# Up projection of a conv-MLP: 19 of 22 channel pairs by seven half-size block products, activation kept in DRAM

## What is computed

```python
h = rms_norm(x, norm_ffn_pre[l])
up = causal_dwconv(jnp.einsum('bsd,df->bsf', h, ffn_w_up[l]), ffn_conv_w[l]) + ffn_conv_b[l]
gate, val = jnp.split(up, 2, axis=-1)
ff = jnp.einsum('bsf,fd->bsd', jax.nn.silu(gate) * val, ffn_w_down[l])
x = x + rms_norm(ff, norm_ffn_post[l])
```

## Time and profile before

| | us |
|---|---|
| three runs: median, lowest, highest | 1058.16, 1056.17, 1058.37 |
| span of the profiled execution | 1058.0 |
| TensorE busy in it | 1044.1 |
| VectorE, ScalarE busy | 492.0, 335.3 |

### The profile page before, as it was taken

The page is one execution under the profiler, slowest core; times in us unless marked ns, Lnnn a source line. Parts: engine busy times, 40 slices in busy tenths (PEclk is TensorE's granted clock), DMA queues, the critical chain, the costliest instruction groups (busy, mean ns, idle before and its releaser), DMA issues.

```text
span 1058.0 us, 12361 instructions
## 1 busy us (share of the span) xinstructions
PE 1044.1 (99%) x4808; PEld 850.6 (80%) x4808; DVE 492.0 (47%) x537; ACT 335.3 (32%) x525; POOL 30.8 (3%) x82
## 2 busy tenths in 40 slices
PE   8999999999999999999999999999999999999997
PEld 7988777768888888888888888888887888888886
DVE  5637776554553443434434343343444233344454
ACT  5425444443332312213121231212223222333342
POOL 2100000001110000000000000000000000000001
PEclk9999999999999999999999999999999999999999
DMA  6521010053232111211112111121211322343343
GB/s 209 146 60 39 23 40 28 33 172 107 94 106 67 57 57 40 59 40 45 54 40 59 40 50 49 40 59 40 79 40 59 100 97 81 99 160 127 131 139 119
DMA packets 75390, 81.59 MB, mean 77 GB/s; under 512 B 2793, under 2 KB 62433, under 8 KB 75361
## 3 DMA queue, kind: packets, MB, share of 16 engines
q1 hardware_dynamic: 75233, 81.13, 24.3%
q0 software_dynamic: 128, 0.07, 0.0%
HBM read 72.80 MB, written 8.39 MB: 77 GB/s over the span
## 4 chain that ended last, share of the span: by engine, by line
PE 95%; DMA 2%; DVE 1%; ACT 1%; issue 0%; POOL 0%; SPq 0%; DVEq 0%; POOLq 0%; ACTq 0%
PE ps L1133 30%; PE ps L1135 30%; PE ps L1134 30%; PE ps L1143 1%; PE ps L1241 1%; DMA xin<-in_x 1%; PE ps L1264 1%; PE ps L1242 1%; PE ps L1250 1%; DMA wraw<-in_w_o 1%; PE ps L1268 1%; DVE hlo L761 0%; PE ps L1279 0%; POOL rstd L449 0%; ACT hhi L486 0%
## 5 line engine op out<-in xcount | busy, mean ns | idle before, releaser
L761 DVE TENSOR_TENSOR wlo<-wraw,whi 128x1024 fp32r<-128x1024 f32 x98 | 120.0, 1224 | 404.6 <-ACT whi L486 404.5
L1133 PE MATMUL ps<-h2hi,whi 128*128 128x512 f32 x704 | 277.5, 394 | 0.0
L1135 PE MATMUL ps<-h2hi,wlo 128*128 128x512 f32 x704 | 276.0, 392 | 0.0
L1134 PE MATMUL ps<-h2lo,whi 128*128 128x512 f32 x704 | 273.2, 388 | 0.0
L486 ACT ACTIVATE whi<-wraw 128x1024 fp32r<-128x1024 f32 x98 | 103.8, 1059 | 513.6 <-PE ps L1135 509.0
L1135 PEld LDWEIGHTS ps<-h2hi,wlo 128*128 128x128 f32 x704 | 132.2, 188 | 30.9
L1134 PEld LDWEIGHTS ps<-h2lo,whi 128*128 128x128 f32 x704 | 132.1, 188 | 29.5
L1133 PEld LDWEIGHTS ps<-h2hi,whi 128*128 128x128 f32 x704 | 132.4, 188 | 26.2
L1133 PE MATMUL ps<-whi,ahi 128*128 128x512 f32 x320 | 126.7, 396 | 0.3 <-DVE alo L1052 0.3
L1135 PE MATMUL ps<-whi,alo 128*128 128x512 f32 x320 | 126.6, 395 | 0.0
L1134 PE MATMUL ps<-wlo,ahi 128*128 128x512 f32 x320 | 126.5, 395 | 0.0
(11 more groups left out here) (135 smaller groups left out, 1015.6 us busy)
## 6 DMA issues: line engine op xcount, KB each, us to landing
wraw<-in_ffn_w_up SPq DMA_DIRECT2D x44, 512.0 KB, 3.8
wraw<-in_ffn_w_down SPq DMA_DIRECT2D x44, 512.0 KB, 3.3
wraw<-in_w_in SPq DMA_DIRECT2D x14, 512.0 KB, 3.9
xin<-in_x SPq DMA_DIRECT2D x8, 512.0 KB, 4.5
wraw<-in_w_o SPq DMA_DIRECT2D x8, 512.0 KB, 3.3
xres<-in_x SPq DMA_DIRECT2D x8, 512.0 KB, 4.1
x_dram<-x2b SPq DMA_DIRECT2D x8, 512.0 KB, 2.9
x2f<-x_dram SPq DMA_DIRECT2D x8, 512.0 KB, 4.1
```

The source lines that it names most:

```text
L761: dve.tensor_tensor(lo[:, slot, :], wraw[:, base % RAW, :], hi[:, slot, :], ALU.subtract).then_inc(w_split, 1)
L1133: pe.matmul(acc, w_hi, x_hi, start=first, stop=False, skip_group_check=looped)
L1134: pe.matmul(acc, w_hi, x_lo, start=False, stop=False, skip_group_check=looped)
L1135: return pe.matmul(acc, w_lo, x_hi, start=False, stop=last, skip_group_check=looped)
```

## The change

Three pairs stay as they were. For the other 19 the pair's product is taken as one of 2 x 2 blocks: token halves by k halves (four blocks of the input) times k halves by gate and value (four blocks of the weight). It is multiplied by seven products (Winograd's form of Strassen's scheme), each one token half, one k half and one block of 128 output channels: 4 x 3 = 12 matmuls of 128x512.

- **Input side.** Four differences of quarters of the input (`r_full`, 128x2048 each) are made once on VectorE, between and after the plain pairs, and rounded and split (`r_hi`, `r_lo`).
- **Weight side.** For each pair VectorE makes four sums of weight quarters (`sum_weights`: one pass of 1024, two of 512); plain and summed quarters are rounded and split as four entries (three of 1024, one of 512) in a ring of six slots (`entry`): `w2hi`, a part of `h2hi` that is read no more, and `whi`.
- **Product side.** Some products serve two outputs. ScalarE copies PSUM to SBUF three times a pair (`keep`, 512 wide), VectorE adds it back to a bank three times (`fold`, 512 wide). TensorE waits before product 3 for the first copy, before product 5 for the third, before product 7 for the second fold. The value comes out negated: its bias is negated (`neg_bias`) and the last product has the factor -1.
- **Activation.** `act_raw` is gone. `yv` has two slots; each finished 128x1024 goes to `act_dram`. The down stage loads 128x512 pieces into a ring of four (`act_in`), the first two early into `gain_a`. `act_in` lies over the input differences, so those loads wait for the last product.
- The loop over pairs is written out on every engine.

The core of the diff:

```diff
+PLAIN = 3
+SEVEN = NF - PLAIN
+RING = 6
+ENTRY_LAST = (4, 5, 6, 7)
...
+            def load_pair(p):
+                for val in range(2):
+                    n = UP0 + 2 * p + val
+                    if p - 2 < PLAIN:
+                        sp.wait_ge(w_split, n - RAW + 1)
+                    else:
+                        sp.wait_ge(u_split, 4 * (p - 2 - PLAIN) + 4)
...
+            def save_act(p):
+                sp.wait_ge(act_ready, p + 1)
+                sp.dma_start(act_dram[p * P:(p + 1) * P, :], yv[:, p % 2, :])\
+                  .then_inc(act_saved[p % 2], 16)
...
+            for p in range(2, NF):
+                load_pair(p)
+                if p >= 3:
+                    save_act(p - 3)
...
+            def keep(q, which):
...
+                act.wait_ge(seven_done, 7 * q + which + 1)
+                if which == 0:
+                    act.wait_ge(act_ready, pair - 1)
+                if which == 2:
+                    act.wait_ge(act_saved[pair % 2], 16 * (pair // 2))
+                out = (yg[:, pair % 2, 0:HALF], yg[:, pair % 2, HALF:], yv[:, pair % 2, 0:HALF])[which]
+                act.activation(out, ps[:, (v0, g1, v0)[which], :], ACT.Copy).then_inc(kept, 1)
...
+            plain_step(0)
+            plain_step(1)
+            round_difference(0)
+            round_entry(0, 0)
+            round_entry(0, 1)
+            plain_step(2)
+            round_difference(1)
+            round_difference(2)
+            round_entry(0, 2)
+            round_entry(0, 3)
+            round_difference(3)
+            for q in range(SEVEN):
+                if q >= 1:
+                    start_value(q - 1)
+                    start_silu(PLAIN + q - 1)
+                if q + 1 < SEVEN:
+                    round_entry(q + 1, 0)
+                for which in range(3):
+                    keep(q, which)
+                if q + 1 < SEVEN:
+                    for i in range(1, 4):
+                        round_entry(q + 1, i)
...
+                start_gate(q)
...
+            def fold(q, which):
...
+                dve.wait_ge(seven_done, 7 * q + 4 + which)
+                dve.wait_ge(kept, 3 * q + 1 + which)
...
+                dve.tensor_tensor(ps[:, (g0, v1, g1)[which], :], ps[:, (g0, v0, g1)[which], :], part,
+                                  ALU.add).then_inc(folded, 1)
...
+            for q in range(SEVEN):
+                pair = PLAIN + q
+                g0, g1, v0, v1 = pair_banks(pair)
+                pe.wait_ge(up_freed, 2 * pair - 2)
+                seventh(q, 1, 0, 0, block_of(h2hi, 0), block_of(h2lo, 0), v0, True)
+                if q == 0:
+                    pe.wait_ge(r_split, 1)
+                seventh(q, 2, 1, 1, r_hi[0], r_lo[0], g1, True)
+                if q == 0:
+                    pe.wait_ge(r_split, 2)
+                pe.wait_ge(kept, 3 * q + 1)
+                seventh(q, 3, 2, 0, r_hi[1], r_lo[1], v0, False)
+                seventh(q, 4, 0, 1, block_of(h2hi, 1), block_of(h2lo, 1), g0, True)
+                if q == 0:
+                    pe.wait_ge(r_split, 3)
+                pe.wait_ge(kept, 3 * q + 3)
+                seventh(q, 5, 1, 0, r_hi[2], r_lo[2], v0, False)
+                seventh(q, 6, 2, 1, block_of(h2hi, 2), block_of(h2lo, 2), g1, False)
+                if q == 0:
+                    pe.wait_ge(r_split, 4)
+                pe.wait_ge(folded, 3 * q + 2)
+                seventh(q, 7, 3, 0, r_hi[3], r_lo[3], v0, False)
```

More of the change, by code:

```diff
@@ L669, in _ @@
             round_h(2 * NT - 1, h2hi)
[L671 to L677, removed]
-                    act.wait_ge(act_ready, pair - 1)
[L679 to L696, removed]
+            def plain_step(p):
+                j = p % 2
+                act.wait_ge(up_done, 2 * p + 1)
+                if p + 1 < PLAIN:
+                    round_weight(UP0 + 2 * p + 2, 0, whi, 0)
+                if p >= 2:
+                    act.wait_ge(act_ready, p - 1)
+                act.activation(yg[:, j, :], banks(4 * j), ACT.Identity, bias=ffn_bias(p),
+                               scale=ffn_tap(2, p)).then_inc(yg_started, 1)
+                act.wait_ge(up_done, 2 * p + 2)
+                if p + 1 < PLAIN:
+                    round_weight(UP0 + 2 * p + 3, 0, whi, 1)
+                if p >= 2:
+                    act.wait_ge(act_saved[j], 16 * (p // 2))
+                act.activation(yv[:, j, :], banks(4 * j + 2), ACT.Identity,
+                               bias=ffn_bias(p + NF), scale=ffn_tap(2, p + NF))\
+                   .then_inc(yv_started, 1)
+                start_silu(p)
@@ L698, in _, with round_act @@
+            def round_act(raw, hi, slot):
+                act.activation(hi[:, slot, :], raw, ACT.Copy).then_inc(a_rounded, 1)
             for q in x2_saved:
                 act.wait_ge(q, 16 * NT // 2)
[L700 to L707, removed]
@@ L719, in _ @@
             d1 = DOWN0 + NF
[L720 removed]
+            a1 = NF - 2
+            down_step(d1, 0, a1)
             for t in (0, 2):
@@ L1055, in low_act, with gate_taps @@
                    .then_inc(a_split, 1)
-            start = steps[0]
-            with dve.Fori(0, NF // 2 - 2) as it:
-                steps[0] = start + 4 * it
-                for j in range(2):
-                    up_step(it + 1, j)
-            steps[0] = start + 4 * (NF // 2 - 2)
-            up_step(NF // 2 - 1, 0)
-            for k in range(2):
-                low_act(k, k, 0, ahi, alo, k)
-            up_step(NF // 2 - 1, 1)
-            def down_step(base, q, k, half):
+            def gate_taps(p):
+                dve.wait_ge(yg_started, p + 1)
+                add_taps(yg[:, p % 2, :], banks(4 * (p % 2)), p)
@@ new lines, in made, with quarter, whole_quarter, low_difference @@
+            def made(i):
+                return r_full[i][:, :, :]
+            def quarter(i, lo):
+                return block_of(h2lo if lo else h2hi, i).rearrange("p t k c -> p t (k c)")
+            def whole_quarter(i, out):
+                return dve.tensor_tensor(made(out), quarter(i, False), quarter(i, True), ALU.add)
+            def low_difference(i):
+                dve.wait_ge(r_rounded, i + 1)
+                dve.tensor_tensor(r_lo[i][:, :, :, :].rearrange("p t k c -> p t (k c)"), made(i),
+                                  r_hi[i][:, :, :, :].rearrange("p t k c -> p t (k c)"),
+                                  ALU.subtract).then_inc(r_split, 1)
```

334 lines of the change are left out of this document (280 added, 54 removed).

## The result

| us | before | after |
|---|---|---|
| median of four runs each, taken side by side | 1058.26 | 1021.10 |
| lowest, highest | 1056.17, 1059.22 | 1019.89, 1022.97 |
| ratio of times, 95% interval | | 0.9645 [0.9627, 0.9663] |
| span of the profiled execution, its own time | 1058.0, - | 1018.1, 1019.89 |

The forecast was 1017.0, range 1011 to 1030. The time is 4.1 us above it, inside the range. In every execution of this study with both on record the time is 1.7 to 2.1 us longer than the span; this is the part around the span, and the forecast could not see it, since the time of before's profiled execution was not known. Before ran in all four, with medians of 1057.5 to 1058.3, so a difference of less than about 1 us between an experiment and the kernel after is no result.

The account below looks back on a forecast made before the run. TensorE, busy 99%, was taken as the bound, so only fewer matmuls save time. Span 1058.0 - 52.1 + 10.3 + 0.6 = 1016.8 us, plus 0.2 to the median: 1017.0, range 1011 to 1030.

Parts of the forecast that it names:

- The 228 matmuls at their spacing, -52.1: Up stage: 19 pairs lose 12 matmuls each, every one worth 0.2287 us of span, 52.1 us less.
- rival 4: Removed matmuls are worth less than their spacing, down to the skill page's 131 ns each: 1039 us; chance 0.01.
- Beside TensorE, cost 0: Seven-product pairs: added VectorE work (15.4 us) and ScalarE work (about 9.0) fit in 19.2 us per pair.
- ring slack: Waits spanning pairs, third fold to copy of product 1: done at 7.5 us, needed at 8.2, slack 0.7.
- Rival 2: Fold or Silu later than taken, so TensorE waits 0.3 to 1 us per pair: 1022 to 1035; chance 0.12.
- rival 3: ScalarE reloads its table at each function swap, 1.9 us stand plus 1.6 low clock per pair: 1080; chance 0.03.
- The start, +10.3: First seven-product pair: late VectorE makes TensorE stand 9.8 us, plus 0.5 for low clock reaching into product 3.
- The seam, +0.6: Start of down stage, k=2: TensorE waits for the act_in load, 0.6 us beyond before's 0.3 (0 to 2).
- DMA, 0: Other loads and saves, including 256 KB more per 5.6 us in the down stage: costed 0.
- One 128x22 negation, below 0.3: Early on, VectorE negates the bias: below 0.3 us, ahead of nothing that TensorE waits for.
- rival 1: Seven-product spacing rises to 0.2328 us, with more waits and busier VectorE: 6.5 us more, about 1023.5; chance 0.14.
- 0.2 between span and time: Whole kernel: 0.2 us from before's span to its median time, added to span 1016.8 to give 1017.0.

Follow-up runs that it names:

- plain9: Kernel after with nine plain pairs instead of three, first entries and differences moved ahead of the last plain pair: 1031.84 us, ratio to before 0.9756.
- plain6: Kernel after with six plain pairs instead of three, first entries and differences moved ahead of the last plain pair: 1022.27 us, ratio to before 0.9669.
- ring3: Kernel after with three more 512-wide ScalarE passes ahead of the first copy out of PSUM, in 14 pairs: 1040.58 us, ratio to before 0.9839.
- dist32: Kernel after with 128 bytes of unused SBUF ahead of gain_a: 1019.85 us, ratio to before 0.9638.
- ring1: Kernel after with one more 512-wide ScalarE pass ahead of the first copy out of PSUM, in 14 pairs: 1021.26 us, ratio to before 0.9663.
- reorder: Kernel after with VectorE and ScalarE work at the start of the seven-product pairs put in another order: 1017.06 us, ratio to before 0.9609.
- align0: Kernel after with 96 bytes of unused SBUF ahead of gain_a: 1005.79 us, ratio to before 0.9512.
- before_align256: Kernel before with 192 bytes of unused SBUF ahead of gain_a: 1046.28 us, ratio to before 0.9882.
- best2: Kernel after with 96 bytes ahead of gain_a, start work ordered by need on VectorE and ScalarE, act_in loads ahead of the last save: 995.38 us.
- order2: Kernel after with start work ordered by need on VectorE and ScalarE, act_in loads ahead of the last save, no added bytes: 1011.73 us.
- align64: Kernel after with 32 bytes of unused SBUF ahead of gain_a: 1015.91 us, ratio to before 0.9601.
- before_align0: Kernel before with 64 bytes of unused SBUF ahead of gain_a: 1067.50 us, ratio to before 1.0079.

## Why the prediction was right

- **The 228 matmuls at their spacing, -52.1.** Right. plain9 less plain6 gives 3.19 us a pair against 12 x 0.2287 = 2.74 plus what the worse placement of the plain ones adds; 131 ns, rival 4, does not fit.
- **Beside TensorE, cost 0.** Right: no stand in any of the pairs behind the first, busy shares as forecast, ring slack 0.66 against 0.7. Rival 2 did not come, but ring3 shows that it was real: 1.9 us more on ScalarE would have eaten half of the gain. One table load for Silu before 350 us and none in 420 to 740: rival 3 has no ground here. ring3 also speaks to its price: a stand of 1 us in each pair did not drop the clock; one of 1.9 us in each was not tried.
- **The start, +10.3.** Right to 0.4: stands of 6.86 and 0.79 against 7.0 and about 1, product 3 late by 9.9 against 9.8. The low clock ended inside product 2 and was hidden behind the wait for `h2lo`, so the 0.5 put in for a low stretch in product 3 did not come.
- **The seam, +0.6.** 0.66, a stand of 0.97. That it came so near is in part luck: with the same code at the seam TensorE stood 1.27 us in dist32, 1.37 in ring1 and 1.41 in reorder, all inside the 0.5 to 1.5 forecast; in align0, where it arrives sooner, 1.65.
- **DMA, 0.** Right for the down stage: 473 matmuls in 110 us at 155 GB/s, and before 0.2328 us at 98 GB/s. At D = 0 it is 487 in 110 us at 153 GB/s (align0, from 772 us) and at 98 GB/s (before_align256). A kernel without the way through DRAM but otherwise like the one after was not run.
- **One 128x22 negation, below 0.3.** This is the step that failed. Its time is small, but its buffer moved the input by 96 bytes and so every `whi` product from 0.2289 to 0.234. With 288 plain matmuls on `whi` at 0.2343 and 504 seven-product ones at 0.2338 that is 288 x 0.0054 + 504 x 0.0049 = +4.0; the other 1092, now at D = 0 and 0.2273 in the mean, gain 1092 x 0.0016 = -1.7. The sum, about +2.3, is an estimate from these spacings. The seven-product stage as a whole hides it (0.2292). So rival 1, that the spacing rises, came true in a small part, but not for the busier VectorE that spoke for it, and most clearly in the plain pairs, where it had not looked.
- **0.2 between span and time.** In the run after it is 1.8. The profiled execution of before, span 1058.0, must have taken about 1059.8 (an estimate, by the 1.8 of the other runs), which is 1.6 over the median and more than any of the four executions in the table. It holds the stand of 2.55 us and the low clock of the earlier trace rows; in the execution after the same place has this row and full clock behind it:
```profile
236.22 0.50 PE L1439 MATMUL ps<-hhi,mhi 128*128 128x512 f32 x1 [1.92 <-DVE hlo L961]
```
So 0.6 of stand and 1.6 of clock, which differ from one profiled execution to the next, were in the base.

Against the forecast span of 1016.8 the measured 1018.1 is 1.3 up. Product 1 started 0.85 late: the three plain pairs took 1.4 us more (68.9 for 67.5, placement), and the up stage began 0.5 earlier than before. This 0.5 is left when the kernel after comes to the stand of the earlier trace rows 1.8 later (52 to 90 us has 179 matmuls for 182, the same placement) and there gets back the 2.2 just told. The start gave 0.4 back. The seven-product pairs, at 0.2294 from start to start for 0.2289, added some 0.8 up to the third down step at 777.32. From that step to the end both kernels take 240.8 us. From the span to this execution's 1019.89 it is the 1.8 around the span, and the median is 1.2 above that, as two of the four executions were 2.4 to 3.1 us longer, at a mean clock of 0.994 and 0.992 for 0.996. Together: 1.3 of span, 1.6 around it (1.8 for 0.2) and 1.2 of median make the 4.1.

## What to carry to other kernels

Price removed matmuls by the spacing that rows of the same operands show, and follow the ring of waits with durations from like rows: that gave each stand of the kernel after to a few tenths. A buffer that is added, dropped or resized moves all that lie behind it: write down the start of the moving and the stationary operand before and after, and if a stage that was not touched changes its pace, look there first. When a stand is removed on one engine, list what else the same product waits for; the next one may be 3 us behind.

## What the runs showed of the hardware

- The time between matmuls of 128x512 goes with the difference of the starts of the two operands modulo 256 bytes: 0.2264 to 0.2268 at 0, 0.2289 at 64, 0.2324 to 0.2345 at the other six places tried, those of the down stage by count. The cost is up to 3.5%. In align0 differences of 95 x 256 bytes (`h2hi` on `whi`) and 256 x 256 bytes (`r_hi` on `w2hi`) are both fast. The place of one operand alone does not decide: in the kernel after, the matmuls with `h2hi` and `h2lo` are 0.2338 to 0.2343 us apart on `whi` and 0.2283 on `w2hi`. That nothing but the difference decides, and why it does, was not shown; starts were moved in steps of 32 bytes only, and the products on `w2hi` reach 0.2285 at D = 0 in the kernel after.
- Load beside TensorE does not move it: align0 and before_align256 start 1414 matmuls in 320 us each, with VectorE at 79% and 41% and DMA at 86 and 49 GB/s.
- Fourteen stands of 1 us, 20 us apart, left the granted clock at 1.00; one of 6.86 us was followed by a low clock up to 402.70. At the place of the earlier trace rows, where every version stands for `hlo`, the clock fell behind 2.55 us (before), 2.60 (reorder), 2.47 (best2), 2.24 (before_align256) and 1.99 (ring3) and did not behind 1.92 (after), 1.86 (order2), 2.09 (align64), 2.49 (before_align0) and 3.05 (plain6): the length of the stand alone does not decide. The Trainium skill (TensorE: Matmul & The Clock Gate, Why this matters for your kernels) asks to avoid idle gaps between bursts of matmuls, as the throughput drops behind them; the falls here agree, and 3.05 us without one shows that it need not. Each fall there costs 1.3 to 1.6 us. It is likely a part of the scatter between executions of one kernel: the four of the kernel after have mean clocks of 0.996, 0.996, 0.994 and 0.992 and spans of 1018.1, 1018.1, 1020.5 and 1021.2 us. Only one execution of each kernel has a trace, so this was not shown.
